# Expert stage of a two-block transformer kernel: the split of the first gate block moved, another home for one gathered row, and two groups of dots taken ahead of the first weighing

## The chip, the core and the metric

The kernel is one program on one core of a Trainium2 chip. The metric is the device time of one execution in microseconds (us); smaller is better. Engines are named as in the profile: PE (matmul) and PEld (its weight load), DVE (vector), ACT (scalar), POOL (GpSimd) and SP (its queue issues most of the weight loads). All transfers run on 16 DMA engines that the queues share.

## What is computed

A first transformer block (three-branch mixer, then a mixture of experts) is followed by a second block of two layers with SwiGLU feed-forwards, a convolution, and attention. 256 tokens of width 1024, all in f32. The change touches the expert part and its border to the first feed-forward:

```python
def chunk(xc):                                   # xc: 128 tokens x 1024
    qh = (xc @ w_q).reshape(Ct, H, 2, 64)        # H = 8 heads
    s = jnp.einsum("nhad,akd->nhak", qh, sub_keys)
    top_s, top_i = lax.top_k(s, K)               # K = 16
    ...
    best_s, pos = lax.top_k(cand, K)
    eidx = jnp.take_along_axis(cand_idx, pos, axis=-1)
    gate = jax.nn.softmax(best_s, axis=-1)
    ug, vg = u_tab[eidx], v_tab[eidx]
    hpre = jnp.einsum("nd,nhkd->nhk", xc, ug)
    act = gate * jax.nn.gelu(hpre, approximate=False)
    return jnp.einsum("nhk,nhkd->nd", act, vg)
```

Each token picks 16 experts per head; each expert is one row of `u_tab` (dotted with the token) and one of `v_tab` (summed with the weight). After it comes `rms_norm`, then the first feed-forward, `swiglu(h, w_gate, w_up, w_down)`.

## The kernel before, in words

**Units.** The expert stage is cut into 16 units: head n of token tile 0 (units 0 to 7), then of tile 1 (8 to 15), 128 tokens each. A unit gathers 16 rows for each token. The table `peer_uv` holds u and v of an expert side by side, so that a row is 2048 words (8 KB) for each of 128 partitions, 1.05 MB in all. The 16 row buffers `rows[0..15]` are one unit's worth; a buffer is gathered into again for the next unit once PE has summed it (semaphore `v_used`). Rows are handled in four groups of four.

**The round of a row group r of unit n.** POOL (`gather`, L679 on) waits for `v_used`, copies four indices (L693), does a carrier operation (L696) and issues four indirect DMAs (L698). DVE takes the dots of the four rows with the tokens (`dots`, L1730) and counts `u_used`. ACT (`weights`, L1051) takes the gelu of the four dots. DVE multiplies by the softmax gate (`weigh`, L1739). ACT writes four diagonal matrices (L1055). PE multiplies each with the v half of its row and sums into PSUM (L2054; 16 records of MATMUL for a group), then counts `v_used`. Between its row groups DVE also finds the experts of unit n + 2: `best_keys` (L1674 and what follows), `best_pairs` (L1683 on) and `best_index` (L1694 on).

**What stands ahead of unit 0.** PE runs the queries and scores of token tile 1 (`query(1, h)`, `later_scores(h)`) and only then turns to the expert sums; `later_scores` counts `panel_used` after heads 1, 3, 5 and 7. With the plan's numbers `FIRST["peer_q"]` is 42 and `FIRST["ffn0"]` is 46, so that 43 means that heads 0 and 1 of tile 1 are through and 46 that all are. ACT copies each query out of PSUM (`query`, L1014), in the order of its own program, then does `split(FIRST["ffn0"])`, then `weights(0)`.

**The first gate block.** The weights of the second block come in panels of 1 MB in three slots `raw[0..2]` in turn, and each is split into a high and a low part: ACT writes `hi` (L753), DVE `lo = raw - hi` (L1314). Panel 46, the first gate block of the feed-forward behind the stage, goes to `raw[1]`. SP issues it (L463) once `panel_used` is 44. ACT's split of it waits for its landing. PE needs it only after the last unit.

**Homes of the late rows.** Buffers 0 to 11 are free early. Of the last four, three lie in what the queries of tile 1 still read, and `raw[late[0]]` (`raw[2]`) held query weights of heads 4 and 5. `raw[late[1]]` is `raw[0]`, which held those of heads 0 and 1. For unit 0 POOL waits for `panel_used` of 46 ahead of the whole last group (`r == EARLY`, L688).

**Order around the change,** written out by hand: on DVE `unit(0, 0, (0, 2))`, `split(46)`, then a loop over units 1 to 5 and the waits and loops behind it. Within `unit`, `weigh(n, 0)` stands ahead of `dots(n, t, 1)`.

Of the kernel before, what the change touches and what calls it, by code (L numbers as in the profile page):

```python
# [49 lines left out]
SLOTS = 3  # L50
PE_HEADS, PE_K, PE_KEYS = 8, 16, 128
# [59 lines left out]
FIRST = {}  # L111
# [59 lines left out]
UNITS = TT * PE_HEADS  # L171
# [9 lines left out]
def build(nc, io):  # L181
    ctx = ExitStack()
    with ctx:
# [14 lines left out]
        raw = [sb(f"raw{s}", [P, PANEL]) for s in range(SLOTS)]  # L198
# [93 lines left out]
        home = [carve(ROW) for _ in range(6)]  # L292
# [1 line left out]
        rows += home[1:4]  # L294
        rows += [over(f"rows_{w}{s}", [P, ROW], f"{w}{s}")[:, :] for w in ("hi", "lo") for s in late]
        rows += [over(f"rows_{w}", [P, ROW], w)[:, :] for w in ("xh", "xl")]
        rows += [home[4], home[5], raw[late[0]][:, :], home[0]]
        EARLY = 3
        wo_hi, wo_lo = (over(f"wo_{w}", [P, PANEL], o, 0, F32R)[:, :] for w, o in (("hi", "oh"), ("lo", "ol")))
        q_last = home[4]  # L300
        xt = home[5].rearrange("p (k t) -> p k t", k=KD)
# [279 lines left out]
        def _(pool):  # L581
# [99 lines left out]
            def gather(n):  # L681

                pool.wait_ge(idx_ready, n + 1)
                for r in range(GROUPS):
                    if isinstance(n, int) and r == 0:
                        pool.wait_ge(panel_used, FIRST["peer_q"])
                    if isinstance(n, int) and r == 1:
                        norm_tile("peer", 1)  # L688
                    if isinstance(n, int) and r == EARLY:
                        pool.wait_ge(panel_used, FIRST["ffn0"])  # L690
                    wait(pool, v_used, PE_K * (n - 1) + GROUP * (r + 1))
                    own = slice(r * GROUP, (r + 1) * GROUP)
                    g.tensor_copy(idx_now[:, own], pe_idx[:, bass.ds(n * PE_K + r * GROUP, GROUP)]).then_inc(idx_copied, 1)  # L693
                    pool.wait_ge(idx_copied, 2 * (GROUPS * n + r) + 1)

                    g.tensor_tensor(pool_carrier, minus_half[:, 0:1], minus_half[:, 0:1], ALU.mult).then_inc(idx_copied, 1)  # L696
                    for k in range(r * GROUP, (r + 1) * GROUP):
                        g.indirect_dma_start(out=rows[k], out_offset=None, in_=io["peer_uv"],  # L698
                                             in_offset=bass.IndirectOffsetOnAxis(ap=idx_now[:, k:k + 1], axis=0))\
                            .then_inc(row_landed[k], 16)  # L700
# [46 lines left out]
        def _(act):  # L747
            def split(p, m=0, i=0):

                s = p % SLOTS  # L750
                act.wait_ge(raw_ready[s], along(LANDED, p, m, i))
                wait(act, panel_used, p + m * i - (SLOTS - 1))
                nc.scalar.activation(hi[s][:, 0:WORDS[p]], raw[s][:, 0:WORDS[p]], ACT.Copy).then_inc(hi_done, 1)  # L753
# [286 lines left out]
            for h in range(PE_HEADS):  # L1040
                query(1, h)
                if h == 3:
                    best_exp(1)
            split(FIRST["ffn0"])

            def weights(n):

# [8 lines left out]

            weights(0)
            best_exp(2)
            with act.Fori(1, UNITS - 2) as n:
                weights(n)  # L1060
                best_exp(n + 2)
            weights(UNITS - 2)
# [237 lines left out]
        def _(dve):  # L1300
# [9 lines left out]
            def split(p, m=0, i=0):  # L1310

                s = p % SLOTS
                dve.wait_ge(hi_done, p + m * i + 1)
                v.tensor_tensor(lo[s][:, 0:WORDS[p]], raw[s][:, 0:WORDS[p]], hi[s][:, 0:WORDS[p]].bitcast(F32), ALU.subtract).then_inc(lo_done, 1)  # L1314
# [352 lines left out]
            def best_keys(n, t, h):  # L1667

                then, sync, done = best_links(n, 0)
                scores = PS[:, :, :].rearrange("p (a g) (h k) -> p a (g h) k", a=2, h=PE_HEADS // 2) if t else pe_sc  # L1670
                own = scores[:, :, bass.ds(h, 1), :].rearrange("p a h k -> p a (h k)")
                if isinstance(n, int) and n == 0:
                    own = PS[:, 0:2, 0:PE_KEYS]
                then(v.tensor_copy(pe_s, own))  # L1674
                sync()
                top16(then, sync, [pe_s[:, a, :] for a in range(2)], [pe_tv[:, a, :] for a in range(2)], [pe_ti[:, a, :] for a in range(2)])
                assert done[0] == BEST_LINKS[0], done

            def best_pairs(n):

                then, sync, done = best_links(n, 1)
                wait(dve, exp_done, n)
                then(v.tensor_copy(pe_tif, pe_ti))  # L1683
                then(v.tensor_tensor(pe_cand, pe_tv[:, 0, :].unsqueeze(2).to_broadcast([P, PE_K, PE_K]),
                                     pe_tv[:, 1, :].unsqueeze(1).to_broadcast([P, PE_K, PE_K]), ALU.add))
                sync()
                top16(then, sync, [pe_cand.rearrange("p i j -> p (i j)")], [pe_best], [pe_pos])
                v.tensor_scalar(pe_nb, pe_best[:, 0:1], -1.0, None, ALU.mult).then_inc(best_ready, 1)
                assert done[0] == BEST_LINKS[1], done

            def best_index(n):

                then, sync, done = best_links(n, 2)
                then(v.tensor_scalar(pe_hl[:, 0, :], pe_pos, 4, None, ALU.logical_shift_right))  # L1694
                then(v.tensor_scalar(pe_hl[:, 1, :], pe_pos, 15, None, ALU.bitwise_and))
                sync()
                then(v.tensor_copy(pe_hlf, pe_hl))
                sync()

                for a in range(2):  # L1700
                    then(v.tensor_tensor(pe_hot[a], iota16[:, :].unsqueeze(1).to_broadcast([P, PE_K, PE_K]),  # L1701
                                         pe_hlf[:, a, :].unsqueeze(2).to_broadcast([P, PE_K, PE_K]), ALU.is_equal))
                sync()
                for a in range(2):
                    then(v.tensor_tensor(pe_hot[a], pe_hot[a], pe_tif[:, a, :].unsqueeze(1).to_broadcast([P, PE_K, PE_K]), ALU.mult))  # L1705
                sync()
                for a in range(2):
                    then(v.tensor_reduce(pe_e[:, a, :], pe_hot[a], AX.X, ALU.add))  # L1708
                sync()
                v.scalar_tensor_tensor(out=pe_idx[:, bass.ds(n * PE_K, PE_K)], in0=pe_e[:, 0, :], scalar=float(PE_KEYS), in1=pe_e[:, 1, :],  # L1710
                                       op0=ALU.mult, op1=ALU.add).then_inc(idx_ready, 1)
                assert done[0] == BEST_LINKS[2], done
# [6 lines left out]
            def gate(n):  # L1719

                dve.wait_ge(exp_done, n + 1)
                v.reciprocal(pe_rec, pe_sum[:, bass.ds(n, 1)]).then_inc(pe_chain2, 1)
                dve.wait_ge(pe_chain2, 2 * n + 1)
                v.tensor_scalar(pe_gate, pe_exp[:, bass.ds(n * PE_K, PE_K)], pe_rec, None, ALU.mult).then_inc(pe_chain2, 1)

            def dots(n, t, r):

                for k in range(r * GROUP, (r + 1) * GROUP):
                    dve.wait_ge(row_landed[k], 16 * (n + 1))
                    v.scalar_tensor_tensor(out=rows[k][:, 0:D], in0=rows[k][:, 0:D], scalar=1.0, in1=xn[:, t, :], op0=ALU.mult, op1=ALU.mult,  # L1730
                                           accum_out=pe_h[:, k:k + 1]).then_inc(u_used, 1)

            def weigh(n, r):

                own = slice(r * GROUP, (r + 1) * GROUP)
                wait(dve, diag_ready, PE_K * (n - 1) + GROUP * (r + 1))
                dve.wait_ge(pe_chain2, 2 * n + 2)
                dve.wait_ge(gelu_done, GROUPS * n + r + 1)
                v.tensor_tensor(pe_act[:, own], pe_gate[:, own], pe_gelu[:, own], ALU.mult).then_inc(act_ready, 1)  # L1739

            def unit(n, t, ahead=None):

                gate(n)
                dots(n, t, 0)
                if ahead:
                    best_keys(n + 2, *ahead)
                weigh(n, 0)
                dots(n, t, 1)
                if ahead:
                    best_pairs(n + 2)  # L1750
                weigh(n, 1)
                dots(n, t, 2)
                if ahead:
                    best_index(n + 2)
                weigh(n, 2)
                dots(n, t, 3)
                weigh(n, 3)
# [9 lines left out]
            dve.wait_ge(pe_sc_ready, 2)  # L1767
            dve.wait_ge(gain_used, TT)
            dve.wait_ge(q_rows, TT)
            unit(0, 0, (0, 2))  # L1770
            split(FIRST["ffn0"])
            dve.wait_ge(pe_sc_ready, PE_HEADS - 1)
            with dve.Fori(1, PE_HEADS - 2) as n:
                unit(n, 0, (0, n + 2))
            dve.wait_ge(panel_used, FIRST["ffn0"])
            with dve.Fori(PE_HEADS - 2, PE_HEADS) as n:
                unit(n, 0, (1, n + 2 - PE_HEADS))
# [886 lines left out]
```

## Time and profile before

| | us |
|---|---|
| median of 3 runs | 2091.26 |
| lowest, highest | 2091.05, 2093.32 |
| profiled execution | 2100.45 |
| its span in the trace | 2098.4 |
| stage, first gather issued to last dot | 386.7 to 1055.3 |

Busy times in the span: PE 1892.0 (90%), PEld 1524.2 (73%), DVE 1283.8 (61%), ACT 772.4 (37%), POOL 415.0 (20%). The 16 DMA engines moved 496.72 MB. The mean granted TensorE clock was 0.946. The profiled execution is 9.2 us longer than the median; durations below come from it.

Read it by stages. PE's 90% is an average over stages in which it sets the pace and one, the expert stage, in which the bytes do. The page's rows of GB/s and of the DMA share, cut into 40 slices of 52.5 us, show which is which.

### The profile page before, as it was taken

The numbers are of one execution on the slowest core, as the hardware profiler recorded it, in microseconds if no ns is written. First come the engines' busy times: TensorE is split into PE (matmuls) and PEld (weight loads), VectorE is DVE, ScalarE is ACT, GpSimd is POOL, SyncE is SP. The second block draws the span as 40 slices with busy tenths as digits, with TensorE's granted clock in tenths as the row PEclk, the third lists the DMA queues.
The fourth block names the chain that finished last, engine by engine and source line by source line (L and its number), as shares of the span: only waits on it lengthen the run. The fifth ranks groups of instructions, "written<-read, shape, count | busy, mean of one in ns | idle before, by whom it ended". The sixth has DMA issues, their size and how long they took to land.

```text
span 2098.4 us, 31012 instructions
## 1 busy us (share of the span) xinstructions
PE 1892.0 (90%) x11358; PEld 1524.2 (73%) x11358; DVE 1283.8 (61%) x2521; ACT 772.4 (37%) x1288; POOL 415.0 (20%) x536
## 2 busy tenths in 40 slices
PE   7999999958778787887789999999999999879998
PEld 7999899823333333333369999999989999769997
DVE  4546855667777767777564556654565445666444
ACT  4346233222222122222134344444354334555333
POOL 4000000346554555555310000000000000110000
PEclk9989999978998998899999999999999999879999
DMA  8323266669999999999946564645546556415552
GB/s 235 98 80 116 67 172 190 251 251 421 422 421 421 422 421 422 422 422 422 422 155 213 186 200 151 201 154 191 186 154 205 193 180 200 141 32 165 185 181 99
DMA packets 231414, 496.72 MB, mean 237 GB/s; under 512 B 21653, under 2 KB 182566, under 8 KB 198566
## 3 DMA queue, kind: packets, MB, share of 16 engines
q1 hardware_dynamic: 188432, 221.36, 33.4%
q0 software_dynamic: 38224, 273.04, 31.5%
q10 hardware_dynamic: 4678, 1.21, 0.3%
q8 instruction: 56, 0.92, 0.2%
q14 instruction: 24, 0.20, 0.0%
HBM read 494.53 MB, written 1.05 MB: 236 GB/s over the span
## 4 chain that ended last, share of the span: by engine, by line
PE 67%; DMA 15%; DVE 8%; issue 5%; POOL 4%; ACT 2%; DVEq 0%; POOLq 0%; ACTq 0%
PE ps L2054 43%; PE acc L2054 23%; DMA rows_xl<-in_peer_uv,idx_now 12%; DMA arena<-in_peer_uv,idx_now 2%; POOL rows_lo L698 1%; POOL rows_xh L698 1%; DVE arena L1701 0%; DVE arena L1705 0%; DVE arena L1708 0%; POOL rstd L613 0%; DVE lo L1314 0%; DVE arena L2003 0%; POOL idx_now L693 0%; POOL arena L698 0%; DVE arena L1530 0%
## 5 line engine op out<-in xcount | busy, mean ns | idle before, releaser
L1314 DVE TENSOR_TENSOR lo<-raw,hi 128x2048 fp32r<-128x2048 f32 x198 | 451.6, 2283 | 311.7 <-ACT hi L753 311.6
L2054 PE MATMUL ps<-xh,hi 128*128 128x256 f32 x1896 | 540.8, 285 | 2.6 <-DVE xl L1335 2.1
L2054 PE MATMUL ps<-xl,hi 128*128 128x256 f32 x1896 | 538.4, 284 | 0.0
L2054 PE MATMUL ps<-xh,lo 128*128 128x256 f32 x1896 | 538.3, 284 | 0.0
L753 ACT ACTIVATE hi<-raw 128x2048 fp32r<-128x2048 f32 x198 | 376.6, 1905 | 276.0 <-PE ps L2054 230.8
L2054 PEld LDWEIGHTS ps<-xh,hi 128*128 128x128 f32 x1896 | 364.9, 192 | 6.0 <-issue 4.4
L2054 PEld LDWEIGHTS ps<-xl,hi 128*128 128x128 f32 x1896 | 365.1, 193 | 1.5
L2054 PEld LDWEIGHTS ps<-xh,lo 128*128 128x128 f32 x1896 | 364.9, 192 | 0.1
L608 POOL TENSOR_SCALAR ss<-ss 128x1 f32<-128x1 f32 x24 | 7.2, 298 | 1005.9 <-ACT arena L1132 879.1
L2054 PE MATMUL acc<-rows,diag 128*128 128x512 f32 x192 | 119.3, 787 | 92.0 <-ACT diag L1055 71.4
L2054 PE MATMUL acc<-arena,diag 128*128 128x512 f32 x384 | 178.7, 605 | 13.9 <-ACT diag L1055 13.9
L2054 PEld LDWEIGHTS acc<-rows,diag 128*128 128x128 f32 x192 | 47.5, 257 | 163.2 <-issue 149.2
L2054 PEld LDWEIGHTS acc<-arena,diag 128*128 128x128 f32 x384 | 73.1, 193 | 112.0 <-issue 83.9
L1730 DVE SCALAR_TENSOR_TENSOR arena<-arena,xn 128x1024 f32<-128x1024 f32 x96 | 115.3, 1223 | 44.6 <-DMA arena<-in_peer_uv,idx_now 44.6
L1055 ACT ACTIVATE diag<-ident,arena 128x128 f32<-128x128 f32 x256 | 81.8, 390 | 156.7 <-DVE arena L1739 149.6
L1051 ACT ACTIVATE arena<-arena 128x4 f32<-128x4 f32 x64 | 13.3, 207 | 325.1 <-DVE arena L1730 164.6
L2054 PE MATMUL acc<-hi,ah 128*128 128x512 f32 x320 | 125.0, 391 | 0.0
L2054 PE MATMUL acc<-lo,ah 128*128 128x512 f32 x320 | 125.0, 391 | 0.0
L2054 PE MATMUL acc<-hi,al 128*128 128x512 f32 x320 | 124.5, 389 | 0.0
L698 POOL DMA_INDIRECT arena<-in_peer_uv,idx_now x96 | 114.0, 1188 | 26.7 <-issue 25.3
L2054 PE MATMUL acc<-rows_lo,diag 128*128 128x512 f32 x128 | 73.8, 730 | 37.5 <-ACT diag L1055 37.5
L2054 PEld LDWEIGHTS acc<-rows_lo,diag 128*128 128x128 f32 x128 | 28.3, 232 | 81.9 <-ACT diag L1055 50.3
(366 smaller groups left out, 3296.8 us busy)
## 6 DMA issues: line engine op xcount, KB each, us to landing
raw<-in_w_ffn_gate SPq DMA_DIRECT2D x44, 1024.0 KB, 5.3
raw<-in_w_ffn_down SPq DMA_DIRECT2D x44, 1024.0 KB, 4.9
raw<-in_w_ffn_up SPq DMA_DIRECT2D x40, 1024.0 KB, 5.4
raw<-in_w_in SPq DMA_DIRECT2D x29, 1024.0 KB, 5.3
raw<-in_w_conv_in SPq DMA_DIRECT2D x11, 1024.0 KB, 5.2
raw<-in_w_kv SPq DMA_DIRECT2D x6, 1024.0 KB, 5.3
raw<-in_w_out SPq DMA_DIRECT2D x4, 1024.0 KB, 5.2
arena<-in_w_ffn_up SPq DMA_DIRECT2D x4, 1024.0 KB, 7.9
```

Source lines behind the costliest of these rows:

```text
L608: g.tensor_scalar(m, m, ss[:, k, TT + t:TT + t + 1], BIAS[name], ALU.add, ALU.add).then_inc(rstd_step, 1)
L698: g.indirect_dma_start(out=rows[k], out_offset=None, in_=io["peer_uv"], in_offset=bass.IndirectOffsetOnAxis(ap=idx_now[:, k:k + 1], axis=0))\
L753: nc.scalar.activation(hi[s][:, 0:WORDS[p]], raw[s][:, 0:WORDS[p]], ACT.Copy).then_inc(hi_done, 1)
L1051: nc.scalar.activation(pe_gelu[:, own], pe_h[:, own], ACT.Gelu).then_inc(gelu_done, 1)
L1055: nc.scalar.activation(diag[:, k % DIAGS, :], ident[:, :], ACT.Copy, scale=pe_act[:, k:k + 1]).then_inc(diag_ready, 1)
L1314: v.tensor_tensor(lo[s][:, 0:WORDS[p]], raw[s][:, 0:WORDS[p]], hi[s][:, 0:WORDS[p]].bitcast(F32), ALU.subtract).then_inc(lo_done, 1)
L1730: v.scalar_tensor_tensor(out=rows[k][:, 0:D], in0=rows[k][:, 0:D], scalar=1.0, in1=xn[:, t, :], op0=ALU.mult, op1=ALU.mult, accum_out=pe_h ...
L2054: return nc.tensor.matmul(out, l, r, start=first, stop=last)
```

## The change

Three edits, none of which changes what is computed. `split(FIRST["ffn0"])` moves on ACT from ahead of `weights(0)` to behind `weights(5)` and `best_exp(7)` (the loop of 13 units is cut in two for it), and on DVE from behind unit 0 to behind unit 5. Of the late rows, row 12 moves to `raw[late[1]]`, rows 13 and 14 to `home[4]` and `home[5]`, and `raw[late[0]]` holds none; for unit 0 the wait moves from the group to the single rows (row 12: 43, rows 13 to 15: 46), so that the four indices are copied ahead of it. On DVE unit 0 is written out with the dots of groups 0 and 1, `best_keys` and `best_pairs` ahead of the first two weighings.

```diff
-        rows += [home[4], home[5], raw[late[0]][:, :], home[0]]
-        EARLY = 3
+        rows += [raw[late[1]][:, :], home[4], home[5], home[0]]
+        EARLY = 12
+        assert late[1] == FIRST["peer_q"] % SLOTS
...
-                    if isinstance(n, int) and r == EARLY:
-                        pool.wait_ge(panel_used, FIRST["ffn0"])
                     wait(pool, v_used, PE_K * (n - 1) + GROUP * (r + 1))
...
                     for k in range(r * GROUP, (r + 1) * GROUP):
+                        if isinstance(n, int) and k >= EARLY:
+                            pool.wait_ge(panel_used, FIRST["peer_q"] + 1 if k == EARLY else FIRST["ffn0"])
...
                 if h == 3:
                     best_exp(1)
-            split(FIRST["ffn0"])
...
             weights(0)
             best_exp(2)
-            with act.Fori(1, UNITS - 2) as n:
+            with act.Fori(1, PE_HEADS - 2) as n:
+                weights(n)
+                best_exp(n + 2)
+            split(FIRST["ffn0"])
+            with act.Fori(PE_HEADS - 2, UNITS - 2) as n:
                 weights(n)
                 best_exp(n + 2)
...
-            unit(0, 0, (0, 2))
-            split(FIRST["ffn0"])
+            gate(0)
+            dots(0, 0, 0)
+            best_keys(2, 0, 2)
+            dots(0, 0, 1)
+            best_pairs(2)
+            weigh(0, 0)
+            weigh(0, 1)
+            dots(0, 0, 2)
+            best_index(2)
+            weigh(0, 2)
+            dots(0, 0, 3)
+            weigh(0, 3)
             dve.wait_ge(pe_sc_ready, PE_HEADS - 1)
             with dve.Fori(1, PE_HEADS - 2) as n:
                 unit(n, 0, (0, n + 2))
+            split(FIRST["ffn0"])
             dve.wait_ge(panel_used, FIRST["ffn0"])
```

## Rows read from the trace of the kernel before

**Rows 1.** The page, part 2: GB/s moved, 40 slices of 52.5 us.

```profile
GB/s 235 98 80 116 67 172 190 251 251 421 422 421 421 422 421 422 422 422 422 422 155 213 186 200 151 201 154 191 186 154 205 193 180 200 141 32 165 185 181 99
```

**Rows 2.** Windows of 10 and 4 us: five engines' busy times, clock, DMA share, GB/s.

```profile
1040.00:1050.00 10.00, 7.20 (x18) 3.03 (x17) 5.17 (x10) 1.49 (x5) 0.00 (x0) 1.00 1.01 422
...
420.00:424.00 4.00, 0.00 (x0) 0.00 (x0) 0.00 (x0) 0.00 (x0) 2.92 (x4) 0.52 1.05 383
...
428.00:432.00 4.00, 0.00 (x0) 0.00 (x0) 0.00 (x0) 0.00 (x0) 0.00 (x0) 0.50 1.01 421
...
436.00:440.00 4.00, 0.93 (x1) 0.50 (x2) 1.63 (x4) 3.52 (x7) 0.00 (x0) 0.50 0.00 0
```

**Rows 3.** Windows of 1 us at both edges of the hole, columns as before.

```profile
432.00:433.00 1.00, 0.00 (x0) 0.00 (x0) 0.00 (x0) 0.00 (x0) 0.00 (x0) 0.50 0.41 168
433.00:434.00 1.00, 0.00 (x0) 0.00 (x0) 0.00 (x0) 0.00 (x0) 0.00 (x0) 0.50 0.16 68
...
452.00:453.00 1.00, 1.00 (x4) 0.50 (x3) 0.97 (x5) 0.00 (x0) 0.70 (x2) 1.00 0.74 106
453.00:454.00 1.00, 1.00 (x3) 0.38 (x2) 0.97 (x5) 0.00 (x0) 0.69 (x2) 1.00 0.48 139
```

**Rows 4.** Timeline of POOL: start, us, line, tile, idle before and its releaser.

```profile
386.69 1.12 POOL L698 DMA_INDIRECT rows<-in_peer_uv,idx_now  x1 [0.17 <-issue]
...
418.53 0.18 POOL L693 COPY idx_now<-arena 128x4 uint32<-128x4 uint32 x1 [12.92 <-PE ps L2054]
...
448.85 0.18 POOL L693 COPY idx_now<-arena 128x4 uint32 x1 [25.02 <-PE acc L2054]
...
450.31 1.81 POOL L698 DMA_INDIRECT rows<-in_peer_uv,idx_now  x1
```

**Rows 5.** The chain that ended last: start, us, what.

```profile
418.44 20.63 issue
439.07 9.60 PE acc L2054 x16
...
490.51 7.15 PE acc L2054 x16
...
850.87 10.22 PE acc L2054 x16
```

**Rows 6.** Timeline of ACT, columns as for POOL.

```profile
417.62 0.28 ACT L1014 ACTIVATE arena<-acc 128x128 f32<-128x128 f32 x1 [2.13 <-PE acc L2054]
434.84 1.91 ACT L753 ACTIVATE hi<-raw 128x2048 fp32r<-128x2048 f32 x1 [16.94 <-DMA raw<-in_w_ffn_gate]
436.77 1.28 ACT L1051 ACT_TABLE_LOAD   x1
...
438.57 1.28 ACT L1055 ACTIVATE diag<-ident,arena 128x128 f32<-128x128 f32 x4 [0.30 <-DVE arena L1739]
```

**Rows 7.** The transfer view, 360 to 500 us: KB each, median us to landing.

```profile
raw<-in_w_ffn_gate SPq DMA_DIRECT2D x1, 1024.0 KB, 24.0
```

**Rows 8.** Timeline of DVE, columns as for POOL.

```profile
409.51 0.15 DVE L1645 COPY arena<-minus_half 128x1 f32<-128x1 f32 x1
438.37 0.17 DVE L1739 TENSOR_TENSOR arena<-arena 128x4 f32<-128x4 f32 x1 [28.71 <-ACT arena L1051]
...
443.03 0.18 DVE L1683 CAST arena<-arena 128x32 f32<-128x32 uint32 x1
...
446.59 1.22 DVE L1730 SCALAR_TENSOR_TENSOR rows_lo<-rows_lo,xn 128x1024 f32<-128x1024 f32 x1
```

**Rows 9.** A window of a quarter us, columns as in the windows above.

```profile
420.00:420.25 0.25, 0.00 (x0) 0.00 (x0) 0.00 (x0) 0.00 (x0) 0.11 (x1) 0.84 0.53 193
```

**Rows 10.** Units 5 and 6: timeline of DVE, columns as for POOL.

```profile
655.82 0.17 DVE L1739 TENSOR_TENSOR arena<-arena 128x4 f32<-128x4 f32 x1 [0.27 <-ACT arena L1051]
...
664.47 1.23 DVE L1730 SCALAR_TENSOR_TENSOR arena<-arena,xn 128x1024 f32<-128x1024 f32 x1 [1.25 <-DMA arena<-in_peer_uv,idx_now]
```

**Rows 11.** The transfer view, 640 to 680 us, columns as before.

```profile
rows<-in_peer_uv,idx_now POOLq DMA_INDIRECT x3, 16.1
```

## The prediction

> **What bounds the kernel now.** I read the page first, its row of GB/s [rows 1]. Eleven slices in a row stand at 421 or 422 GB/s and no other slice comes near: from about 472 to 1049 us the kernel moves bytes as fast as it ever does. That is the expert stage, and there neither PE nor DVE sets the pace. Its bytes are fixed: 16 units of 16 rows of 1.05 MB. What can change is only how long the DMA engines stand idle between the first gather and the last. So the second view is the windows. The last full one of the stage still shows a share of 1.01 and 422 GB/s [rows 2], and the 59 windows of 10 us from 460 to 1050 all look like it (417 to 426). Ahead of that they are full from 392 to 432, then nothing [rows 2], then full again from 454 on. The hole's edges come from the windows of 1 us [rows 3]: the bytes after 432 are worth (168 + 68) / 421 = 0.56 us at full rate, so the engines run out at 432.56; those before 454 are worth (106 + 139) / 421 = 0.58 us, so they are back at 453.42. **The hole is 20.9 us**, and since all behind it runs at the rate of the bytes, it stands in the kernel's time in full.
>
> The third view is who ends the hole. POOL's first index copy for unit 1 waited 25.02 us for PE and came at 448.85, its first gather at 450.31 [rows 4]: unit 1 can't be gathered before PE has used the four rows of unit 0's first group. The chain puts those sums at 439.07 for 9.60 us, and 20.63 us of "issue" ahead of them [rows 5]. That word means only that the profile matched no releaser. ACT's timeline gives it: four diagonals from 438.57, so the first is written by 438.57 + 1.28 / 4 = 438.89, and PE starts 0.18 us later. And ACT was there so late because it stood 16.94 us for the landing of the gate block, split it, and only then loaded the gelu table [rows 6]. That block took 24.0 us to land [rows 7], since it was issued into full queues. DVE had been waiting for the gelu for 28.71 us [rows 8]. The chain of the hole is thus: gate block lands, ACT splits, gelu, weigh, diagonals, PE, POOL.
>
> **The split moved on ACT** takes the first two links away. ACT's last query copy ends at 417.62 + 0.28 = 417.90 [rows 6]. Everything that the gelu of group 0 needs is there: DVE ended its dots and `best_keys` by 409.66 [rows 8]. From the start of the table load to the first diagonal took 438.57 - 436.77 = 1.80 us, to PE's first sum 439.07 - 436.77 = 2.30 us. So PE starts at 417.90 + 2.30 = 420.2 instead of 439.07. PE's own work ahead of it ended at 418.44 [rows 5], so it doesn't hold this up.
>
> ACT ran the table load 0.02 us after the split's ACTIVATE ended (434.84 + 1.91) and nothing stood between [rows 6]. Against this speaks the Trainium skill, "ScalarE: Activation LUTs", section "What ACT_TABLE_LOAD costs": a switch of tables costs a drain of some 1.38 us beside the load's 1.28. By that rule PE would start at 421.6 and the saving below would be 1.4 us smaller; the row shows no such drain, and the sum goes by the row.
>
> **The price of the first 16 sums** has three rows [rows 5]: 9.60 us as they ran here, 7.15 at the full clock, 10.22 at the worst. The granted clock left 2.4 GHz for 1.2 GHz in the quarter ahead of 420.25 (0.84 is two thirds of it at the upper level, so at 420.17) [rows 9], 1.7 us after PE's last matmul; the new start at 420.2 comes just behind that. I take 9.60, the row for this very place, which began at the lower clock too; 7.15 and 10.22 are the bounds. PE ends the group at 429.8 (427.4; 430.4). The index copy followed PE's end by 0.18 us before, and full rate came 453.42 - 448.85 = 4.57 us after the copy. The engines are then full again at 434.5 (432.1; 435.2).
>
> Against that, when do they run out? The bytes ahead are the same, so at 432.56, less a dip between 420 and 424 (383 GB/s, worth 4 x 38 / 421 = 0.36 us [rows 2]) that the next edit fills: 432.2. **The hole shrinks from 20.9 us to 2.3** (0; 3.0). Saving 20.9 + 0.4 - 2.3 = **18.9 us** (21.2; 18.2).
>
> **Is the next group late then?** Group 1's sums follow group 0's on PE without a pause if its diagonals stand by 429.8. DVE goes from 409.66 into the dots of group 1, four of some 1.15 us, if those rows have landed: the first gather was issued at 386.69, the restart shows 453.42 - 450.31 = 3.1 us from issue to full rate, and eight rows of 1.05 MB take 20 us at 421 GB/s, so row 7 is there by 409.8. They end at about 414.4. `best_pairs` takes 446.59 - 443.03 = 3.6 us [rows 8] with a weighing of 0.1 in it, so till 418. ACT's gelu is what comes last (419.5), the second gelu waits for the four diagonals, and group 1's diagonals stand by about 423. At 7.15 us a group PE then ends its groups near 437, 444 and 451, each gathered 10 us of bytes per group: the second batch must be moving by 444.5 and is by 437 + 4.6 = 441.7. The queue then only gets longer. Nothing reopens the hole.
>
> **Dots ahead of the weighing**, by itself, is worth about nothing. In the old order DVE would reach group 1's dots at 419.6, end them at 424.2, and group 1's diagonals would stand near 426, still ahead of 429.8. At the full clock (427.4) the margin is 1 us, so I price this edit at 0 to 1 us. Without the first edit it gives nothing: the same gelu is waited for.
>
> **Row 12 elsewhere.** The last group's index copy came at 418.53 after 12.92 us for PE's scores [rows 4]. Now the copy and row 12 follow row 11 at about 407 and rows 13 to 15 come at 418.5. The queues are full anyway, so what it brings is the dip, 0.36 us, counted above. Behind the moved wait stands nothing else on POOL but unit 1, which waits for PE. The homes exchanged are of the same size.
>
> **The split at its new place** costs ACT 1.9 us and DVE 2.3, and makes DVE wait for ACT. In unit 5 DVE's last weighing is at 655.82 [rows 10]. ACT then has four diagonals (1.28), a table load (1.28), an exp (0.5) and the split (1.91): 5.1 us with the gaps, till 661.0; DVE's part lasts till 663.3, `gate` till 664.1. Unit 6's first dots would go from there, and the last of that group's rows was waited for till 664.47 [rows 10], so they end at 668.7 instead of 665.7: 3.0 us late. All behind it on DVE, ACT, PE and POOL shifts by 3. What hides it is the queue of gathers: the first rows of a unit are issued 16.1 us before they land [rows 11], against some 3.1 + 2.5 = 5.6 us in empty queues, so they lie about 10 us ahead of need. 3.0 of 10: cost 0. If that cover were gone it would be 3.0 us, once.
>
> **Sum.** The trace's 2098.4 us of span and 2100.45 of time become 2079.5 and 2081.55. The median of the runs is 9.2 us below the profiled execution; no row says that the hole differs in them, so I take the same 18.9 us off it: 2091.26 - 18.9 = **2072.4**.
>
> **Rivals.**
>
> *The clock stays up.* PE's pause is 1.8 us and its new start stands within 0.1 us of the fall of the clock. Then group 0 costs 7.15 us, the hole is gone, and the time is 2091.26 - 21.2 = 2070.1. Chance 0.25.
>
> *Late rows hold the first weighing.* The new order puts `weigh(0, 0)` behind the dots of group 1. Should rows 4 to 7 land ten us later than by rate (the gate block took 24.0 us in the same queues [rows 7]), the weighing, PE and the restart all go back by about as much: half the saving, 2081.6. For it speaks that a queue shares with others; against it, that only these gathers were in it until the gate block was issued at 434.84 - 24.0 = 410.8. Chance 0.07.
>
> *PE's "issue" is real.* The chain's 20.63 us [rows 5] might be PE or ACT waiting for code and not for the diagonal. Instructions come through the same 16 engines, and a transfer issued into them at 410.8 took 24.0 us. PE would again not start before the queues are empty, and the time stays 2091. For it: nothing but the word; against it: the 0.18 us between diagonal and sum. Chance 0.05.
> The Trainium skill has that mechanism in "Runtime: NRT & Kernel Launch", section "Instruction fetch mechanics": a taken branch to code that is not at hand waits for a fetch. The change adds a loop on ACT; no row here shows what a branch costs in full queues.
>
> *The lead is lost (slower).* In the kernel before, all of unit 0 was worked off in the hole, and the loop started with idle engines and a full set of rows. If the round of a row group (dot, gelu, weigh, diagonal, PE, POOL) took longer than its queue lasts, each unit from 1 on would end with a small hole. The place to see it is POOL's wait for PE ahead of a unit's first gather; the price is 15 times the shortfall, and it decides from 18.9 / 15 = 1.3 us a unit: at 1.6 us the time is 2072.4 + 24 = 2096. Against it stands the lead of 10 us in units 5 and 6 [rows 11]. Chance 0.03.
>
> **How the numbers follow.** 0.60 for the forecast (2072.4; 2073.1 with the 10.22 us row, 2074.1 if the dots' order costs its 1 us the other way), 0.25 for 2070.1, 0.07 for 2081.6, 0.05 for 2091, 0.03 for slower. The runs before lie 2.3 us apart, so each end gets 1.5 us more: 2070.1 - 1.5 = 2068.6 and 2074.1 + 1.5 = 2075.6. The 0.15 of the last three rivals is what lies outside. 0.2% is 4.2 us, about what a measurement of this kernel can tell from no change. Faster: 0.60 + 0.25 + 0.07 = 0.92; same 0.05; slower 0.03.
>
> **What would show it.** Right: ACT's gelu table load at 417.9 and PE's first sum near 420.2; no row of ACT waiting for the gate block; POOL's copy for unit 1 at 427.5 to 430.5; DMA windows full from 392 on but for at most 3 us near 433; the last dot near 1036; DVE's `lo` split in unit 6 with a wait for `hi` of some 5 us before it, and full windows around it. Wrong: PE's first sum later than 423; a dip in GB/s after unit 5; POOL's waits for PE gone while DMA windows fall under 415; or the stage 19 us shorter and what follows longer.

## The result, and the profile after

| | before | changed |
|---|---|---|
| median of 3 runs, us | 2091.26 | 2079.72 |
| lowest, highest | 2091.05, 2093.32 | 2079.22, 2080.98 |
| profiled execution | 2100.45 | 2080.98 |
| its span | 2098.4 | 2079.2 |
| last dot of the stage ends | 1055.3 | 1037.5 |

The ratio is 0.9941, with a 95% interval of 0.9926 to 0.9957: 11.5 us, or 0.6%, faster. The prediction said 2072.4, in a range of 2068.6 to 2075.6. The sign is right and the time lies 4 us above the range. The two profiled executions, however, lie 19.5 us apart, and the prediction's sum for them (2081.55 of time, 2079.5 of span) stands within 0.6 us of what the changed kernel shows. So two things have to be explained: that the mechanism came out as worked out, and that the median moved 8 us less.

The page of the changed kernel, part 2, answers to [rows 1]. The ninth slice (420 to 472 us before; 416 to 468 us here, where a slice is 52.0 us) has gone from 251 to 395, and the run of full slices ends sooner (373, then 189):

```profile
GB/s 238 97 80 112 73 173 173 243 395 422 422 422 422 421 421 422 421 422 422 373 189 188 182 202 145 189 179 190 188 168 187 187 190 187 142 45 158 182 184 99
```

Its windows of 1 us at the edges of what is left of the hole, with the columns of [rows 2] (clock, DMA share and GB/s last), answer to [rows 3]:

```profile
432.00:433.00 1.00, 1.00 (x3) 0.38 (x2) 1.00 (x1) 0.00 (x0) 0.85 (x2) 1.00 0.45 172
433.00:434.00 1.00, 1.00 (x4) 0.45 (x3) 0.10 (x2) 0.00 (x0) 0.96 (x1) 1.00 0.14 50
434.00:435.00 1.00, 1.00 (x4) 0.50 (x3) 0.87 (x1) 0.00 (x0) 0.74 (x1) 1.00 0.80 115
435.00:436.00 1.00, 1.00 (x3) 0.38 (x2) 0.53 (x3) 0.30 (x2) 1.00 (x1) 1.00 0.47 180
```

The engines run out at 432 + (172 + 50) / 421 = 432.5 and are back at 436 - (115 + 180) / 421 = 435.3: a hole of 2.8 us where it had been 20.9.

ACT's timeline (start, us, line, operation, idle before and its releaser) answers to [rows 6]. No row waits for the gate block; the table load follows the last query copy by 0.02 us:

```profile
417.97 0.28 ACT L1015 ACTIVATE arena<-acc 128x128 f32<-128x128 f32 x1 [2.13 <-PE acc L2069]
418.27 1.28 ACT L1051 ACT_TABLE_LOAD   x1
419.56 0.21 ACT L1051 ACTIVATE arena<-arena 128x4 f32<-128x4 f32 x1
420.07 1.28 ACT L1055 ACTIVATE diag<-ident,arena 128x128 f32<-128x128 f32 x4 [0.30 <-DVE arena L1743]
```

The chain in the window 415 to 470 us answers to [rows 5]. 20.63 us of "issue" have become 1.78, and two groups of sums take 15.68:

```profile
418.80 1.78 issue
420.57 15.68 PE acc L2069 x32
```

POOL's timeline answers to [rows 4]. The copy for unit 1 comes at 429.57 (before: 448.85), within the 427.5 to 430.5 forecast:

```profile
429.57 1.28 POOL L692 COPY idx_now<-arena 128x4 uint32 x1 [7.07 <-PE acc L2069]
430.93 1.07 POOL L695 TENSOR_TENSOR arena<-minus_half 128x1 f32<-128x1 f32 x1
432.15 1.81 POOL L699 DMA_INDIRECT rows<-in_peer_uv,idx_now  x1
```

DVE's timeline shows the split at its new place, with the wait of 5 us that was forecast, and the windows of 10 us around it show that it costs no bytes:

```profile
642.89 2.29 DVE L1318 TENSOR_TENSOR lo<-raw,hi 128x2048 fp32r<-128x2048 f32 x1 [4.93 <-ACT hi L754]
```

```profile
640.00:650.00 10.00, 5.77 (x14) 2.28 (x12) 6.95 (x10) 4.13 (x5) 8.78 (x7) 1.00 1.01 418
650.00:660.00 10.00, 4.96 (x6) 2.18 (x7) 9.56 (x39) 1.70 (x6) 2.83 (x3) 0.52 1.01 421
660.00:670.00 10.00, 10.00 (x24) 4.39 (x23) 9.15 (x32) 1.49 (x5) 3.37 (x4) 0.97 1.01 420
```

### The profile page after: what moved, and what is told of

It reads as the page before. It is cut to its first block, busy times and chain, and to the rows that moved or that the text cites. A ratio compares the mean times of both kernels' runs of the same rounds, so it can differ in the third digit from the quotient of the medians.

```text
span 2079.2 us, 31013 instructions
## 1 busy us (share of the span) xinstructions
PE 1890.2 (91%) x11358; PEld 1523.0 (73%) x11358; DVE 1283.7 (62%) x2521; ACT 771.6 (37%) x1288; POOL 416.3 (20%) x536
## 3 DMA queue, kind: packets, MB, share of 16 engines
HBM read 494.53 MB, written 1.05 MB: 238 GB/s over the span
## 4 chain that ended last, share of the span: by engine, by line
PE 68%; DMA 14%; DVE 8%; POOL 4%; issue 4%; ACT 2%; DVEq 0%; POOLq 0%; ACTq 0%
PE ps L2069 43%; PE acc L2069 24%; DMA rows_xl<-in_peer_uv,idx_now 11%; DMA arena<-in_peer_uv,idx_now 3%; POOL rows_lo L699 1%; POOL arena L699 1%; POOL rows_xh L699 1%; POOL rstd L614 0%; DVE lo L1318 0%; DVE arena L1705 0%; DVE arena L1709 0%; DVE arena L2018 0%; DVE arena L1712 0%; POOL idx_now L692 0%; DVE arena L1534 0%
## 5 line engine op out<-in xcount | busy, mean ns | idle before, releaser
L2069 PE MATMUL acc<-arena,diag 128*128 128x512 f32 x384 | 172.3, 595 | 7.6 <-ACT diag L1055 7.6
L699 POOL DMA_INDIRECT arena<-in_peer_uv,idx_now x96 | 111.5, 1161 | 38.3 <-issue 26.4
```

What stands on the lines that cost most here:

```text
L2069: return nc.tensor.matmul(out, l, r, start=first, stop=last)
```

## The experiments

Twelve runs of ten kernels followed, in four sets, each on one chip and beside the kernel before. "Ratio" is to the kernel before in the same set, with the 95% interval. None of the ratios is 2% from 1: all these are differences of a fraction of a percent, told apart by their intervals. Two measures are used below. The *landing* is the time from SP's issue of the gate block to its landing, from the transfer view. The *hole* is what the window from 424 to 462 us lacks of full rate: 38 x (1 - GB/s / 421) us; a window of 419 or 418 GB/s counts as 0.2 or 0.3 by it.

### Where do the 8 us sit that the medians lack?

Both kernels again, no edit.

> The kernel before, unchanged, with a profile of its own beside the timed runs. Theory 1 (the hole varies): in executions near 2091 us the gate block lands earlier than the 24.0 us of the profiled execution, ACT's split starts near 426 instead of 434.8, and the hole is about 12 us instead of 20.9; everything outside the hole is as in the trace of 2100.45 us. Theory 2 (the rest varies): the hole is 20.9 us in every execution, and the 9 us between 2100.45 and 2091.26 lie in other stages. Theory 3 (an odd execution): the hole is 20.9 us and the others agree with 2100 too, the 2091 being the exception.

> The changed kernel, unchanged, beside the kernel before on one chip. Theory 1: about 11 to 12 us below before where before runs near 2091, with PE's first sum at 420.6 and a hole of 2 to 3 us, as in its trace. Theory 2: its own executions vary by 9 us as before's do. Theory 3: 19 us below.

The kernel before: median 2095.78 in 12 runs, from 2089.43 to 2100.65; 19 more runs of it beside this set gave 2093.3, from 2088.41 to 2098.4. The changed kernel: 2078.84 in 6 runs, from 2078.28 to 2080.94; ratio 0.9937 (0.9923 to 0.9951). It is the kernel before that varies, by 12 us, on one chip. Its second trace is of an execution of 2090.07 us, where the gate block landed 13.4 us after its issue and not 24.0 as in [rows 7]. ACT's timeline, the transfer view and the window of 424 to 462 us of that execution:

```profile
424.38 1.91 ACT L753 ACTIVATE hi<-raw 128x2048 fp32r<-128x2048 f32 x1 [6.35 <-DMA raw<-in_w_ffn_gate]
```

```profile
raw<-in_w_ffn_gate SPq DMA_DIRECT2D x1, 1024.0 KB, 13.4
```

```profile
424.00:462.00 38.00, 30.84 (x65) 13.55 (x66) 32.57 (x98) 13.32 (x31) 20.00 (x18) 0.86 0.73 292
```

ACT splits 10.5 us sooner than in [rows 6], and the hole is 38 x (1 - 292 / 421) = 11.6 us. The span is 2088.2: 10.2 us less, of which the hole accounts for 9.3. Theory 1 holds for this execution (the split comes 1.6 us sooner than it said); theories 2 and 3 fall. Beside these longer series the change is worth 14.5 us (2093.3 to 2078.84), and in a later set 16.0 us (2095.13 to 2079.14, ratio 0.992, 0.9908 to 0.9932): the three runs behind 2091.26 had fallen at the low end of what the kernel before does.

### Which of the three edits carries the gain?

The split alone (the other two edits as before), and the changed kernel with the split put back:

```diff
 # e1_split_only, on the kernel before: ACT and DVE
-            split(FIRST["ffn0"])          # ahead of weights(0); behind unit 0
+            split(FIRST["ffn0"])          # behind weights(5), best_exp(7); behind unit 5
```

> Of the three edits the moved split alone: rows and their waits and the order of unit 0 on DVE as before. By the prediction's sum it carries all of the gain but 0.4 us (the dip) and 0 to 1 us (the order): within 1.5 us of the changed kernel. Rival (the order of the dots carries a part): DVE reaches group 1's dots only at 419.6 and PE pauses between the first two groups; 3 us or more above the changed kernel.

2079.0 us in 6 runs (2078.55 to 2083.16), ratio 0.994 (0.9925 to 0.9955), against 2078.84 of the changed kernel in the same set. The split carries all of it; rows and order together are worth 0.2 us, less than can be told.

> The changed kernel with the split back at its old places on ACT and DVE: the homes of the rows and the order of the dots alone. By the prediction: the gelu still waits for the gate block, so the hole and the time are those of the kernel before, within 1 us. Rival (the other two edits matter by themselves): more than 2 us below before.

2098.64 us in 8 runs, ratio 1.003 (1.0018 to 1.0042): 5 us *slower* than the kernel before, and narrow (2097.57 to 2101.8). Neither theory said that. In its trace the block lands after 23.3 us. Either the rows or the order had to do it, so each ran alone:

```diff
 # e3_row12_only, on the kernel before
-        rows += [home[4], home[5], raw[late[0]][:, :], home[0]]
+        rows += [raw[late[1]][:, :], home[4], home[5], home[0]]   # and its waits, as in the change
```

> Of the three edits the rows alone, on the kernel before: row 12 issued at 406 and not at 419. Theory (the gate block's landing sets the hole, and it lands early only where the queue of rows runs out of rows for a moment): row 12 keeps that queue filled, so the block always lands some 23 to 24 us after its issue; 2098 to 2100 us with a narrow spread, as the changed kernel with the split put back (2098.64). Rival (the order of the dots is what made that one slow): 2088 to 2100 with the wide spread of the kernel before.

2100.66 us in 11 runs (2097.32 to 2103.28), ratio 1.0019 (1.001 to 1.0028), beside 2096.84 for the kernel before in that set (2093.19 to 2102.46). Slower by 4 us; the spread of 6 us is wider than expected, though it starts where the other's middle is. What spreads it is not shown. Transfer view and window of its trace:

```profile
raw<-in_w_ffn_gate SPq DMA_DIRECT2D x1, 1024.0 KB, 24.3
```

```profile
424.00:462.00 38.00, 24.69 (x52) 10.72 (x53) 24.24 (x64) 11.86 (x26) 13.21 (x11) 0.77 0.46 178
```

> Of the three edits the order of unit 0 on DVE alone, on the kernel before. Theory: it can't move the gelu, which waits for the gate block; the wide spread of the kernel before, 2088 to 2100, and the same median within 3 us. Rival of the run above: always near 2098.

(`e4_order_only`: unit 0 on DVE as in the change, all else as before.) 2094.39 us in 11 runs (2090.93 to 2099.38), ratio 0.9991 (0.9979 to 1.0002): no difference, the wide spread kept, as expected. Landing in its trace 20.2 us, hole 18.1 us.

So row 12 by itself makes the landing late. In the kernel before POOL issues the last four rows from 419 on [rows 4], just when the first twelve run out. The queues' rows (packets, MB, share of the engines' time; q0 carries the gathers, q1 the gate block) show what the block gets out of that moment. The kernel before, first trace, 420 to 424 us:

```profile
q1 hardware_dynamic: 717, 0.72, 55.0%
q0 software_dynamic: 116, 0.81, 50.3%
```

Row 12 alone, 414 to 429 us:

```profile
q0 software_dynamic: 741, 5.42, 87.4%
q1 hardware_dynamic: 742, 0.76, 15.1%
```

With row 12 in the queue (issued at 404.36 in this trace) the gathers never run dry, and in 15 us the two queues move one packet each in turn, 741 and 742. In the kernel before most of the block slips through in a gap of 3 us. The block's packets, of 1040, in windows of 3 us:

| kernel | 417-420 | 420-423 | 423-426 | 426-429 | 429-432 | 432-435 | landing us |
|---|---|---|---|---|---|---|---|
| row 12 alone | 146 | 149 | 151 | 148 | 208 | 5 | 24.3 |
| before, first trace | 150 | 683 | 44 | 19 | 9 | 8 | 24.0 |
| order alone | 163 | 702 | 16 | 9 | 5 | 0 | 20.2 |
| before, second trace | 163 | 739 | 21 | 0 | 0 | 0 | 13.4 |

The kernel before thus has its block nearly through when the last four rows come in, in both traces: 80 packets, 8%, are left at 423 in one and 21 in the other. Those 80 take 12 us more. So the late landings have two shapes: a steady share (row 12 alone) and a short tail that the last rows hold up (the kernel before). A tail of 3 packets per us (9 from 429 to 432) is what one of the 16 engines alone would move, since all of them together move 742 in 15 us; that it is one engine with its part unfinished is an estimate from these counts, and no row shows the engines singly.

### Is it those four rows that hold the block?

The kernel before with the late rows held until the block has landed:

```diff
                         pool.wait_ge(panel_used, FIRST["ffn0"])
+                        pool.wait_ge(raw_ready[FIRST["ffn0"] % SLOTS], LANDED[FIRST["ffn0"]])
```

> The kernel before, but unit 0's last four rows are gathered only once the gate block has landed, so that nothing new can get in beside it. Theory (the spread of the kernel before is whether these rows, issued at 419, get into the queues before the block is through): the block lands 13 to 14 us after its issue in every execution, the time is 2088 to 2091 with a spread under 3 us, below the median of the kernel before although the rows come 5 us later. Rival (the landing varies for a reason of its own, memory or other queues): the spread of 10 us stays.

2091.04 us in 8 runs, from 2088.61 to 2091.9, ratio 0.9976 (0.9966 to 0.9986): the spread falls from 7 us (2091.39 to 2098.74 for the kernel before in this set) to 3.3, and a wait *added* makes the kernel 4 us faster. The spread is a little over the 3 us expected. The tail is gone: 589 packets of the block pass from 420 to 423 us, 204 in the next 3, none behind. Transfer view and window (here the hole holds a gap between the twelfth row and the thirteenth too, since the last four are issued from 426.61 on):

```profile
raw<-in_w_ffn_gate SPq DMA_DIRECT2D x1, 1024.0 KB, 14.3
```

```profile
424.00:462.00 38.00, 30.01 (x64) 12.79 (x64) 31.26 (x94) 12.31 (x27) 23.73 (x23) 0.87 0.78 301
```

### Does the landing set the hole, and the packet the landing?

A quarter of the block, and the whole of it in runs of 8 KB instead of 1 KB:

```diff
 # e5_quarter_block                  (f == 0 only)
-                load(p0, column(gate, 0))
+                load(p0, gate[0:2 * P, 0:PC].rearrange("(k p) n -> p k n", p=P))
 # e8_wide_block                     (f == 0 only)
-                load(p0, column(gate, 0))
+                load(p0, gate[0:P, 0:PANEL].rearrange("p (k n) -> p k n", k=KD))
```

> The kernel before with only a quarter of the first gate block loaded (256 of its 1024 rows; the rest of the slot keeps what was there, so that much of the feed-forward's weights is left out); the split stays where it was and is as long as before. Theory: a quarter lands before ACT is through with the queries (417.9), so ACT splits at once, PE's first sum comes at 422.2 and the queues are full again at 436.5, and 0.79 MB less is moved (1.9 us): about 2083 us, spread under 3 us. Rival (the hole isn't set by the landing but by the split's place itself, or by PE's own start): above 2088.

2085.95 us (2085.93 to 2087.81), ratio 0.9949 (0.9934 to 0.9964), spread 1.9 us. The theory's direction and spread hold; the time is 3 us above it, and so is PE's first sum (425.01 for 422.2), since even a quarter was not there by 417.9. ACT still waited for it, till 420.79; it landed 9.8 us after the issue:

```profile
420.79 1.91 ACT L753 ACTIVATE hi<-raw 128x2048 fp32r<-128x2048 f32 x1 [2.76 <-DMA raw<-in_w_ffn_gate]
```

> The kernel before with the first gate block's 1 MB read in runs of 8 KB (128 rows of 2048 columns, so that wrong weights go into that block) and not in runs of 1 KB; issue, size, split and all else are as before. Theory (beside the gathers the block gets a turn per packet, so that packets of 1 KB get a ninth of the rate and 8 KB would get half): 1.05 MB at some 210 GB/s land 7 to 9 us after the issue, before late rows can matter; ACT splits at 418 to 420, the hole is 5 to 7 us, about 2083 us with a spread under 3 us. Rival (the share doesn't depend on the packets): it lands after 13 to 24 us as before and the time and spread stay.

2086.27 us (2082.54 to 2087.09), ratio 0.9946 (0.9932 to 0.9959). The same 1.05 MB landed after 9.4 us, at 144 packets and not 1040, as the queue's rows from 405 to 450 us say (packets, MB, share), here those of this kernel:

```profile
q1 hardware_dynamic: 144, 1.05, 5.6%
```

```profile
raw<-in_w_ffn_gate SPq DMA_DIRECT2D x1, 1024.0 KB, 9.4
```

The counts of both queues from 415 to 419 us are equal here too, at eight times the bytes for the block:

```profile
q1 hardware_dynamic: 111, 0.91, 54.6%
q0 software_dynamic: 112, 0.79, 47.2%
```

The share depends on the packets. The landing (9.4 us for 7 to 9), the hole (7.5 for 5 to 7), the time (3 us above) and the spread (4.6 us for under 3) all miss the expectation a little, but the rival falls.

Landing, hole and span of all traced executions in which ACT waits for the block:

| kernel | landing us | hole us | span us |
|---|---|---|---|
| row 12 alone | 24.3 | 21.9 | 2095.8 |
| before, first trace | 24.0 | 20.9 | 2098.4 |
| split back | 23.3 | 21.1 | 2096.7 |
| order alone | 20.2 | 18.1 | 2093.9 |
| rows behind block | 14.3 | 10.8 | 2088.4 |
| before, second trace | 13.4 | 11.6 | 2088.2 |
| quarter block | 9.8 | 8.7 | 2084.6 |
| wide block | 9.4 | 7.5 | 2084.6 |

In the changed kernel the block lands after 23.2, 23.4 and 26.4 us in three traces, as late as where ACT waits or later, and nobody waits: spans 2079.2, 2078.5 and 2075.0, holes 3.0, 1.8 and 0.2. Span less hole is 2074 to 2078 in all of these. Two more traces in which nobody waits leave 2079: the split alone (landing 19.2, hole 0.5, span 2079.5) and the first of the kernel of the next section (landing 26.3, hole 0.2, span 2079.2). What lies outside the hole thus varies by 5 us between executions: the first gather is issued at 384.6 to 387.6 us, and 1040.3 to 1045.0 us follow the last dot. The table shows how hole and landing go together, but no single span is good to better than that.

### Can the last 3 us of the hole be had?

The changed kernel with the gelu of unit 0's first group ahead of the last query copy, once by itself and once beside the changed kernel on one chip:

```diff
             for h in range(PE_HEADS):
+                if h == PE_HEADS - 1:
+                    gelu(0, 0)
                 query(1, h)
```

> The changed kernel with one step more: ACT takes the gelu of unit 0's first group ahead of the copy of the last query, so that its table load (1.28 us) lies in the 2.1 us that ACT waits for PE there. Theory: DVE's first weighing then comes at 418.1 instead of 419.9, PE's first sum at 418.9 instead of 420.6, right behind its last score, the clock stays at its upper level, the 16 sums take 7.15 us and not 9.0, and the last 2.8 us of the hole go: 2.0 to 2.8 us below the changed kernel. Rival (the hole moves on to the next late step, or the clock falls all the same): 0 to 1.5 us below.

> The changed kernel once more, on the chip of the run below, for comparison with it: 2079 us, within 1 us of its earlier median.

> The changed kernel with the gelu of unit 0's first group ahead of the last query copy, beside the changed kernel on one chip. Theory (the 2.6 us that the stage gets shorter at its start are partly given back at its end, where the last 16 sums fell on the lower clock, 8.85 us for 7.15): 0.5 to 1.5 us below the changed kernel. Rival (that fall is luck of one execution): 2 to 2.8 us below.

First set: 2078.88 us (2077.82 to 2080.91), where the changed kernel had 2078.84 in another set, on another chip. Second set: 2080.88 us (2078.47 to 2082.78) against 2079.14 (2076.04 to 2080.3) for the changed kernel. No gain either time: both expectations missed. The step does what it should at its own place. In the second trace the gelu is taken while PE works and the sums follow PE's last score; ACT's and PE's timelines:

```profile
416.46 1.28 ACT L1032 ACT_TABLE_LOAD   x1
417.75 0.21 ACT L1032 ACTIVATE arena<-arena 128x4 f32<-128x4 f32 x1
```

```profile
419.32 5.42 PE L2076 MATMUL acc<-rows,diag 128*128 128x512 f32 x12
```

12 of the first 16 sums take 5.42 us, at the upper level of the clock, and the hole is 0.3 us. But in the third trace of the changed kernel the clock stayed up by itself, at the same idle of 1.8 us, and its hole is 0.2 us too:

```profile
418.30 5.39 PE L2069 MATMUL acc<-rows,diag 128*128 128x512 f32 x12 [1.77 <-issue]
```

in place of 7.08 us from 420.57 in the first. So the step had in both of its traces what the changed kernel has in some executions. At the end of the stage the clock differs by execution too. The chain of the changed kernel's third trace has the last 16 sums of the stage at 8.85 us and not 7.15:

```profile
1034.46 8.85 PE acc L2069 x16
```

Why the shorter hole does not show in the time is open in part. From first gather to last dot the stage takes 650.5, 649.5 and 648.8 us in the three traces of the changed kernel, 649.4 and 648.8 with the step: of 2.8 us of hole at most 1.7 are seen at the stage's end, and what follows the last dot varies more than that (1045.0 and 1040.3 us in the step's two traces). The third trace of the changed kernel also owes 2.3 of its 4.2 us to an earlier start of the stage (384.77 for 387.04). What remains, 1.7 us in favour of the changed kernel with overlapping runs, isn't told apart by these runs. No version that ran beats the changed kernel.

## Why the prediction was wrong, and where it was right

**The hole and its chain: right.** 20.9 us, ended by gate block, split, gelu, weigh, diagonals, PE, POOL. All experiments that moved the landing moved the hole, as long as ACT waited for it. The stage became 18.2 us shorter between the two profiled executions (668.7 to 650.5 us, first gather to last dot).

**PE's new start: right.** Forecast 420.2, measured 420.57, with the last query copy 0.35 us later than in the first trace. The drain of 1.38 us that the Trainium skill, "ScalarE: Activation LUTs", "What ACT_TABLE_LOAD costs", adds to a table load is not seen in the changed kernel either: 417.97 + 0.28 = 418.25, load at 418.27, gelu at 419.56. The measurement decides against it here.

**The 16 sums: right within their bounds.** Forecast 9.60 with 7.15 as the other end. The first trace has 8.8 (15.68 less 6.9 for the second group), the third 7.15. The reason given for 9.60 was wrong, however: that the sums would begin at the lower clock, since it had fallen at 420.17. In the changed kernel's first trace the granted clock is still 1.00 when the sums begin at 420.57; the window from 421.5 to 422 has 0.73, so that it falls near 421.7, and it is up again by 425.5. The rival "the clock stays up" was real in the third trace; it isn't one kernel's property.

**The rest of the hole: right, partly by luck.** Forecast 2.3 us (0 to 3.0), measured 2.8, 1.8 and 0.2. In the first trace PE starts 0.4 us late, the sums are 0.8 us short, and from the index copy to full rate it takes 435.3 - 429.57 = 5.7 us, not 4.57, since POOL issues the first gather 2.6 us behind the copy and not 1.5; the errors offset each other.

**Next groups, the split at its new place: right.** The DVE wait of 4.93 us and full windows around it (418 to 421 GB/s). The queue of gathers that was to cover it was there. The last dot came at 1037.5, for a forecast near 1036.

**The order of the dots: right,** nothing that can be measured.

**Row 12: wrong in kind.** I priced it as a gain of 0.36 us, as the filling of a dip between 420 and 424 us. [rows 2] has a DMA share of 1.05 in that dip, so the engines weren't idle there: 0.72 MB of the gate block went through in packets of 1 KB and took 55.0% of their time, where the gathers' 0.81 MB took 50.3%. With the split moved, rows and order together are worth nothing that can be told. On the kernel before it costs 4 us, since it keeps full the queue beside which the gate block has to get through. I counted the bytes and left out who waits for whose.

**The step that failed** stands under "Sum": "the median of the runs is 9.2 us below the profiled execution; no row says that the hole differs in them, so I take the same 18.9 us off it". The gain is the length of a wait for a transfer in a contended queue, and such a wait need not be the same twice. In the traced execution of 2090.07 us it is some 10 us shorter (landing 13.4 for 24.0). What the change removes, down to the 2.8 us that are left, is therefore about 9 us in that execution and 18 in the first. The executions behind the median of 2091.26 have no traces; that their holes were short is inferred from that one. The row was there: a landing of 24.0 us for 1 MB in [rows 7], against 5.3 for the same size elsewhere on the page, says that the term is contention. And the 9.2 us between profiled execution and median were a warning that I set aside. Since the change takes the contended wait out of the path, the trace's own sum was the forecast to give: 2100.45 - 18.9 = 2081.55, where 2079.72 was measured. That it stands so close is partly luck, since what lies outside the hole varies by 5 us. Part of the miss is the draw of three runs, too: taken off the kernel before's median of a later set (2095.13), the same 18.9 us give 2076.2, where that set has 2079.14. Subtracting a term from a time in which the term has another size was the error.

**The rivals.** *Late rows hold the first weighing*: no, the dots of rows 4 to 7 ran back to back from 409.93 to 414.5. *PE's "issue" is real*: no; PE started in full queues, 0.18 us behind the first diagonal. The rule of fetches behind a taken branch (the Trainium skill, "Runtime: NRT & Kernel Launch", "Instruction fetch mechanics") shows no price in these rows: where ACT leaves its first loop, table load, exp and split follow each other from 639.37 to 642.86 without a pause of more than 0.05 us. Whether any branch here needed a fetch is not shown. *The lead is lost*: no, the window of 436 to 1030 us holds 422 GB/s on the mean.

## What to carry to other kernels

Before a saving is taken off a median, ask whether the term that goes is a constant (an instruction) or a wait for something shared; in the second case its size in the profiled execution is one draw, and the kernel without it is forecast from that same execution and not from the median. A difference between the profiled execution and the median is a finding about some wait, to be assigned before it is subtracted. And a transfer that somebody waits for in program order is at the mercy of a bulk stream beside it: here, filling that stream better made the kernel slower, and moving the consumer to where the data had long landed made the landing time stop mattering.

## What the runs showed of the hardware

A transfer of 1.05 MB in runs of 1 KB got one packet for each packet of the gathers in runs of 8 KB that stood in another queue: 742 and 741 in 15 us (row 12 alone), 0.76 MB or 51 GB/s for the one, 5.42 MB or 361 GB/s for the other. The same bytes in runs of 8 KB had equal counts as well, 111 and 112 in 4 us, and with them half of the bytes (0.91 and 0.79 MB); they landed in 9.4 us. A quarter of the block in runs of 1 KB took 9.8. The share thus goes by packets and not by bytes or by transfers. Each of these landings holds some 3.5 us before the block's first packet moves: an estimate from row 12 alone, where 85 packets, 1.7 us at that rate, had moved by 414, 5.2 us after the issue at 408.79.

The Trainium skill, "DMA: Bandwidth & Descriptors", "Queues, rings and completion order", says that an engine takes turns between the queues that have work, a packet at a time. An estimate from that rule, a turn of 1 KB for each of 8 KB, is a ninth, 47 GB/s; the steady windows, with 51 GB/s, agree. How many runs such a turn holds is not shown: equal counts come out if it is the same number in both queues. The 24.0 us of the kernel before (44 GB/s on the mean) look like the same share but are not: two thirds of the block went through in 3 us and the last 8% took 12.

When the gathers ran dry for a moment, the block moved 683 to 739 packets in 3 us instead of 149.

TensorE's granted clock left its upper level (2.4 GHz) 1.7 us after PE's last matmul in both traces of the kernel before and with the quarter block, but 4.8 to 5.0 us after it with the split back, with row 12 alone, with the order alone, with the rows behind the block and with the wide block, at the same place of the program. In the changed kernel an idle of 1.8 us was followed by a fall 1.1 to 1.2 us into the sums in two traces (7.08 us for 12 of them) and by none in a third and in the split alone (5.39). The same gap thus costs 0 or 1.7 us by execution.
